# Turning a stage's rows in float32r from a copy made by transfers

## The chip, the cores and the metric

The kernel runs on one core of one Trainium2 chip. Its engines are TensorE (PE, with weight loads shown as PEld), VectorE (DVE), ScalarE (ACT), GpSimd (POOL) and SyncE (SP); each works through its own list of instructions and waits on semaphores. The metric is the device time of one execution in microseconds; lower is better.

## The reference

A model of one sequence of 256 tokens with 1024 features, all float32. Three layers follow each other:

```
h = x
h += attention(rmsnorm(h));           h += relu(rmsnorm(h) @ w1)**2 @ w2      # layer 0: mix0, mlp0
h += rglru_block(rmsnorm(h));         h += relu(rmsnorm(h) @ w1)**2 @ w2      # layer 1: mix1, mlp1
x = rmsnorm(h);  hn = rmsnorm(x)                                              # pre
u = hn @ w_in                                       # 11352 columns: gla, dsa, cross, gates
merged = s_gla*(gla @ w_g) + s_dsa*(dsa @ w_d) + s_mem*(cross(mem) @ w_x)
out = x + rmsnorm(merged @ w_o)
```

What matters here is that the result of each stage has tokens on its rows, and the next product needs it with features on its rows. So between two stages a 256 x 1024 array is turned.

## The kernel before, in words

**Products.** Weights come in tiles of 128 partitions x 2048 float32 (1 MB). `PLAN` is the list of all tiles in the order of their use, `T_OF[name, i]` a tile's place in it. Each tile is cut in two: `hi`, the weights rounded to float32r (ACT, line 852), and `lo = raw - hi` (DVE, line 1379), both by half tiles. The other operand is cut likewise (`xh`, `xl`, side by side in `X2`), and a product is the sum of high x high, low x high and high x low, all in float32r. `raw` has five buffers (`RAW`), `hi` three (`HIS`); `lo` is written over `raw`.

**Loads.** SP issues the load of tile u in plan order, each after the tile five places before is used up (`load`, line 2073 is its `dma_start`). Other transfers of SP stand between two loads at fixed places.

**The order.** PE's instructions are written out by hand. `half(name, i, j, x, b, ks)` makes the 128 output features j of tile i from the blocks `ks` of 8 input feature blocks: a high matmul of 512 columns and a low one of 256 for each. `tokens(name, i, x, banks, ts)` makes tokens x 512 columns from four blocks, three matmuls of 512 columns for each block and each half of the tokens; `rows` is the same for tiles cut by input features. `cols_as_ready` starts a stage: it takes the eight feature blocks in order and waits for each `x_low`. The tiles `mk` and `mv` belong to the product with `mem`, which depends on no stage; they are placed at the stage entries so that PE has work while the stage's input is made.

**Stage entries.** There are five. At mlp0 and mlp1 the rows `h` are turned as soon as DVE has added the stage before (`add_rows`, `h_added`, one increment for 128 tokens x 512 features, order (s 0, c 0), (s 1, c 0), (s 0, c 1), (s 1, c 1)). At mix1 and pre `hn`, the rows times their norm, are turned (`normed`, `hn_made`). At the end `merged` is turned in two halves of the features c. Function `turned` (line 503) waits for the rows, and turns them by 128 x 128 blocks: `PE.transpose` (line 514) with the float32 unit matrix `ident`, four blocks to a bank, two banks to a half c. `turned_x` does both halves. ACT then reads each bank with the norm's gain into `xh` (`x_highs`, line 931), DVE subtracts for `xl` (`x_lows`, line 1415); for `merged` these are `f_highs` (line 1339) and `f_lows` (line 1976). DVE's order at the end is: fl of half 0, `lo` of wf 1, `merged` of half 1 (`to_m`), fl of half 1, then `lo` of wf 2 and wf 3.

Of the kernel before, what the change touches and what calls it, by code (L numbers as in the profile page):

```python
# [8 lines left out]
P = 128  # L9
S = 256  # L10
D = 1024
NC = D // P
F32 = mybir.dt.float32
F32R = mybir.dt.float32r
ALU = mybir.AluOpType
ACT = mybir.ActivationFunctionType
AX = mybir.AxisListType.X

RAW, HIS, BT = 5, 3, 3
# [42 lines left out]
T_OF = {key: t for t, key in enumerate(PLAN)}  # L62
# [28 lines left out]
def build(nc, A, out):  # L91
    ctx = ExitStack()

    def sem(name):
        return ctx.enter_context(nc.semaphore(name))
# [7 lines left out]
    ones_in, vec_in, ident_in, gmask_in, mem_in, h_in = (  # L103
        sem("ones_in"), sem("vec_in"), sem("ident_in"), sem("gmask_in"), sem("mem_in"), sem("h_in"))
# [2 lines left out]
    toep_in, toep2_in, toep_cut = [sem(f"toep_in{i}") for i in range(4)], sem("toep2_in"), sem("toep_cut")  # L107
    first_in, warm_set, kq_scaled, q_scaled, mk_scaled, tok_made = (
        [sem(f"first_in{i}") for i in range(5)], sem("warm_set"), sem("kq_scaled"), sem("q_scaled"), sem("mk_scaled"), sem("tok_made"))
    eps_set, v_step, a_step = sem("eps_set"), sem("v_step"), sem("a_step")  # L110
    x_high, x_low = sem("x_high"), sem("x_low")
    sq_made, sq_added, rstd_made = sem("sq_made"), sem("sq_added"), sem("rstd_made")
# [40 lines left out]
    def slot(name, i, free=(NC, S), dt=F32, off=0):  # L153
        return place(name, o_slot[i] + off, free, dt)

    def small(name, free, dt=F32):
        n = 4
        for f in free:
            n *= f
        return place(name, region((n + 31) // 32 * 32), free, dt)  # L160

    vec = small("vec", [NV])
    ones = small("ones", [P])
    ident = small("ident", [P])
    gmask = small("gmask", [P])
    o_sq = region(4 * 1024)
    o_tmp = region(5 * 1024)
# [77 lines left out]
    gP = slot("gP", 13, [D])  # L245
    fh, fl = slot("fh", 6, dt=F32R), slot("fl", 7, dt=F32R)
    res = slot("res", 9, [2, D])

    bank = [ctx.enter_context(nc.psum_tensor(f"bank{i}", [P, 512], F32)) for i in range(8)]

# [14 lines left out]
    def low_at(name, k_):  # L265
        return NC * SPLITS.index(name) + k_ + 1
# [4 lines left out]
    def pe():  # L271
# [167 lines left out]
            else:  # L439
                used(t, m)  # L440

        def tokens(name, i, x, banks, ts=(0, 1)):
            t = T_OF[name, i]
            c, part = i // 2, i % 2
            wh, wl = hi[t % HIS], lo[t % RAW]
            for s_, k_ in [(s_, k_) for s_ in ts for k_ in range(4)]:
                b = banks[s_]
                if part == 0 and k_ == 0:
                    fill((name, c, s_), b)
                p.wait_ge(lo_cut, cut_at(t, k_ // 2))  # L450
                w, r = slice(k_ * 512, (k_ + 1) * 512), slice(s_ * P, (s_ + 1) * P)
                kk = 4 * part + k_
                m = mm3(bank[b][:, :], x[0][:, kk, r], x[1][:, kk, r], wh[:, w], wl[:, w],
                        part == 0 and k_ == 0, part == 1 and k_ == 3)
                if part and k_ == 3:
                    m.then_inc(filled[b], 1)
            if ts[-1] == 1:
                if part:
                    tile_end[t] = full[name, c, 1]
                else:  # L460
                    used(t, m)
# [41 lines left out]
            PE.matmul(o, V[:, 0, a:b], PT[n % 2][:, 0:256], start=True, stop=False)  # L503
            return PE.matmul(o[:, P:S], V[:, 1, a:b], PT[n % 2][:, 256:384], start=False, stop=True)

        def turned(name, src, c, ready, banks, read):

            p.wait_ge(*ready)
            for m_ in range(2):
                b = banks[m_]  # L510
                done = fill(("turned", name, 2 * c + m_), b, read[m_])
                for e in range(4):
                    j, s_ = 4 * c + 2 * m_ + e // 2, e % 2
                    m = PE.transpose(bank[b][:, e * P:(e + 1) * P], src[:, s_, j * P:(j + 1) * P], ident[:, :])  # L514
                m.then_inc(done, 1)

        def turned_x(name, src, ready, n0):
            for c in range(2):
                turned(name, src, c, (ready, n0 + 2 * c + 2), (2 * c, 2 * c + 1),
                       [(x_low, low_at(name, 4 * c + 1)), (x_low, low_at(name, 4 * c + 3))])  # L520

        X, M = (xh, xl), (mh, ml)

# [68 lines left out]
        def mlp(n, fill_i):  # L592
            p.wait_ge(x_low, low_at("mem", NC - 1))
            half("mk", fill_i, 0, M2, 7)
            turned_x(f"mlp{n}", h, h_added, 8 * n)
            half("mk", fill_i, 1, M2, 6)
            for i in range(17):
                if i == 0:
                    cols_as_ready(f"w1_{n}", 0, X2, (4, 5), f"mlp{n}")
                elif i < 16:  # L600
                    cols_by_part(f"w1_{n}", i, X2, (6, 7) if i == 1 else (4, 5))
                if i > 0:
                    p.wait_ge(z_low, 32 * n + 2 * i)
                    rows(f"w2_{n}", i - 1, 16, zh[(i - 1) % 3], zl[(i - 1) % 3])
# [1 line left out]
        mlp(0, 0)  # L606
        half("mk", 1, 0, M2, 7)
        half("mk", 1, 1, M2, 6)
        half("mk", 2, 0, M2, 4, range(0, 4))
        turned_x("mix1", hn, hn_made, 0)  # L610
        half("mk", 2, 0, M2, 4, range(4, 8))
        half("mk", 2, 1, M2, 5)

        def gates(n):
            p.wait_ge(xc_made, n + 1)
# [19 lines left out]

        tokens("mv", 2, M, (7, 6))
        tokens("mv", 3, M, (7, 6), (0,))
        turned_x("pre", hn, hn_made, 4)
        tokens("mv", 3, M, (7, 6), (1,))

        cols_as_ready("iq", 0, X2, (4, 5), "pre")
        half("misc", 0, 0, X2, 0, last=True)
# [164 lines left out]
        X2_ = (xh2, xl2)  # L807
        for n in range(3):
            tokens("wx", n, X2_, (6, 7) if n < 2 else (4, 5))
        turned("merged", merged, 0, (merged_made, 2), (6, 7), [(f_low, 1), (f_low, 2)])  # L810
        tokens("wx", 3, X2_, (4, 5))

        def last_rows(i):
            p.wait_ge(f_low, i + 1)
            rows("wf", i, 4, fh[:, 2 * i:2 * i + 2, :], fl[:, 2 * i:2 * i + 2, :])

        last_rows(0)
        turned("merged", merged, 1, (merged_made, 4), (4, 5), [(f_low, 3), (f_low, 4)])
        last_rows(1)
        for s_, c in ((0, 0), (0, 1), (1, 0), (1, 1)):  # L820
            r = slice(s_ * P, (s_ + 1) * P)
            for i in (2, 3):
# [9 lines left out]
    def act():  # L832
# [43 lines left out]
        def second(*key, scale=1.0, func=ACT.Copy, **kw):  # L876
            n = len(order)
            order.append(key)
            bt_at[key] = n
            a.wait_ge(*full[key])  # L880
            if n >= BT:
                a.wait_ge(*free[order[n - BT]])
            ACTE.activation(bt[n % BT][:, :], bank_of[key][:, S:2 * S], func, scale=scale, **kw).then_inc(bt_made, 1)  # L883
# [92 lines left out]
        at_tile("wq", 0)  # L976
        for j in range(2):
            second("wq", j, scale=0.125)

        def turned_pair(n):  # L980
            if n >= 2:
# [1083 lines left out]
    def sp():  # L2065
        SP = nc.sync
        s = Side(SP)

        def load(u_):
            name, i = PLAN[u_]  # L2070
            if u_ >= RAW:
                s.wait_ge(*tile_end[u_ - RAW])
            SP.dma_start(raw[u_ % RAW][:, :], A[name][i]).then_inc(raw_in[u_ % RAW], 16)

        SP.dma_start(first[:, :], A["first"][:, 0:3 * S + 16]).then_inc(first_in[0], 16)
        SP.dma_start(second_[:, :], A["second"]).then_inc(first_in[1], 16)
        for k_ in range(3):
            SP.dma_start(front[k_][:, :], A["front"][:, k_, :]).then_inc(first_in[k_ + 2], 16)
        SP.dma_start(hx[:, 4:NC, :], A["xT"]).then_inc(x_in, 16)
        SP.dma_start(vec[:, :], A["vec"]).then_inc(vec_in, 16)  # L2080
        load(2)
        SP.dma_start(ones[:, :], A["ones"]).then_inc(ones_in, 16)
        SP.dma_start(ident[:, :], A["ident"]).then_inc(ident_in, 16)
        SP.dma_start(gmask[:, :], A["gmask"]).then_inc(gmask_in, 16)
        load(3)
        load(4)
        SP.dma_start(mem[:, :, :], A["memT"]).then_inc(mem_in, 16)
        for u_ in range(5, TILES):
            load(u_)
            if 5 <= u_ < 9:  # L2090
                i = u_ - 5
                SP.dma_start(T[:, 4 * i:4 * i + 4, :], A["T"][:, 4 * i:4 * i + 4, :]).then_inc(toep_in[i], 16)
            if u_ == T_OF["wo", 0]:
                SP.dma_start(h[:, :, :], A["x"].rearrange("(s p) d -> p s d", p=P)).then_inc(h_in, 16)
            if u_ == T_OF["w1_0", 8]:
                SP.dma_start(bo[:, :], bass.AP(A["bo"].tensor, 0, [[0, P], [1, D]])).then_inc(bo_in, 16)
            if u_ == T_OF["w1_1", 8]:
                SP.dma_start(gF[:, :], bass.AP(A["gF"].tensor, 0, [[0, P], [1, D]])).then_inc(gf_in, 16)
            if u_ == T_OF["wf", 0]:
                s.wait_ge(ox_gated, 4)  # L2100
                SP.dma_start(gP[:, :], bass.AP(A["gP"].tensor, 0, [[0, P], [1, D]])).then_inc(gp_in, 16)
        for n in range(4):
            s_, r = half_of(n // 2, n % 2)
            s.wait_ge(res_made, n + 1)
            SP.dma_start(out[s_ * P:(s_ + 1) * P, r], res[:, s_, r]).then_inc(out_done, 16)
        s.wait_ge(out_done, 4 * 16)
# [93 lines left out]
```

## Time and profile before

| | |
|---|---|
| three runs | 977.17, 976.54, 976.76 us; median 976.76 |
| profiled execution | 976.28 us, its span 975.0 us |
| mean granted TensorE clock | 0.999 |
| busy | PE 99%, PEld 85%, DVE 70%, ACT 60%, POOL 7% of the span |
| moved | 180.33 MB, 185 GB/s over the span |

The span runs from the first to the last instruction; the profiled execution's time has a little more around it. In a timeline row the instructions of a line that follow each other are put together: the first number is the first one's start, the second reaches from there to the last one's end. A matmul's end is modelled, and matmuls are pipelined: the distance between two starts is what one costs, not its duration.

### The profile page before, as it was taken

What the parts mean: (1) busy time and instruction counts of PE and PEld (TensorE: products, weight loads), DVE (VectorE), ACT (ScalarE), POOL (GpSimd) and SP (SyncE); (2) the same over time, 40 slices, a digit from 0 to 9 for tenths busy, and PEclk for the clock granted to TensorE, in tenths of its full rate; (3) what the DMA queues carried; (4) which work ended last, traced back from release to release, by engine and by line L of the source; (5) the groups of instructions that cost most, each with busy time, mean ns of one, the idle gap of its engine ahead of it and who ended that gap; (6) DMA issues with size and microseconds to landing.
All of it is one profiled execution on the core that took longest, in us unless ns stands there. A gap on an engine that the chain in (4) does not pass through costs nothing.

```text
span 975.0 us, 13399 instructions
## 1 busy us (share of the span) xinstructions
PE 968.3 (99%) x5146; PEld 826.5 (85%) x5146; DVE 680.5 (70%) x1161; ACT 589.0 (60%) x1042; POOL 66.1 (7%) x80
## 2 busy tenths in 40 slices
PE   9999999999999999999999999999999999999997
PEld 6887788888888898888888888888888888988886
DVE  5887776665667789666665688778767554877564
ACT  6777755454456897645454466547876555684443
POOL 1323110000000242000000000000011000000000
PEclk9999999999999999999999999999999999999999
DMA  9753545655455445545555556455553544335551
GB/s 367 301 197 132 181 173 189 222 178 210 173 203 183 148 159 196 182 184 189 222 178 211 173 204 245 171 175 193 194 169 103 195 146 169 133 130 210 175 191 44
DMA packets 27119, 180.33 MB, mean 185 GB/s; under 512 B 2992, under 2 KB 3888, under 8 KB 6320
## 3 DMA queue, kind: packets, MB, share of 16 engines
q1 hardware_dynamic: 26336, 176.98, 50.8%
q0 software_dynamic: 288, 2.10, 0.6%
q8 instruction: 41, 0.67, 0.3%
q10 hardware_dynamic: 432, 0.39, 0.1%
q14 instruction: 22, 0.18, 0.0%
HBM read 178.41 MB, written 1.05 MB: 184 GB/s over the span
## 4 chain that ended last, share of the span: by engine, by line
PE 99%; DMA 1%; DVE 0%; ACT 0%; SPq 0%; issue 0%; DVEq 0%
PE bank L293 16%; PE bank L295 16%; PE bank L294 16%; PE bank L338 14%; PE bank L366 11%; PE bank L346 7%; PE bank L372 6%; PE bank L308 1%; PE bank L498 1%; PE bank L514 1%; PE bank L619 1%; PE bank L548 1%; PE bank L309 1%; PE bank L559 1%; DMA front<-in_front 1%; PE bank L434 0%
## 5 line engine op out<-in xcount | busy, mean ns | idle before, releaser
L1379 DVE TENSOR_TENSOR lo<-raw,hi 128x1024 fp32r<-128x1024 f32 x318 | 376.0, 1230 | 20.1 <-ACT hi L852 19.9
L852 ACT ACTIVATE hi<-raw 128x1024 fp32r<-128x1024 f32 x318 | 320.2, 1050 | 100.1 <-PE bank L295 98.2
L338 PE MATMUL bank<-X,hi 128*128 128x512 f32 x536 | 141.8, 397 | 0.0
L883 ACT ACTIVATE bt<-bank 128x256 f32<-128x256 f32 x135 | 51.2, 382 | 140.6 <-PE bank L372 66.3
L366 PE MATMUL bank<-X,hi 128*128 128x512 f32 x480 | 118.8, 390 | 0.0
L338 PEld LDWEIGHTS bank<-X,hi 128*128 128x128 f32 x536 | 96.7, 189 | 16.9
L366 PEld LDWEIGHTS bank<-X,hi 128*128 128x128 f32 x480 | 90.2, 188 | 17.6
L1393 DVE TENSOR_TENSOR zr<-bank,bt 128x256 f32<-128x256 f32 x64 | 27.2, 424 | 108.4 <-ACT bt L883 108.4
L293 PE MATMUL bank<-hi,zh 128*128 128x512 f32 x256 | 100.0, 390 | 0.0
L295 PE MATMUL bank<-hi,zl 128*128 128x512 f32 x256 | 99.8, 390 | 0.0
L294 PE MATMUL bank<-lo,zh 128*128 128x512 f32 x256 | 99.6, 389 | 0.0
L346 PEld LDWEIGHTS bank<-X,lo 128*128 128x128 f32 x536 | 73.1, 190 | 5.4
L346 PE MATMUL bank<-X,lo 128*128 128x256 f32 x536 | 74.7, 282 | 0.0
L293 PE MATMUL bank<-hi,X 128*128 128x512 f32 (+1 forms) x176 | 67.9, 386 | 0.0
L295 PE MATMUL bank<-hi,X 128*128 128x512 f32 (+1 forms) x176 | 66.9, 380 | 0.0
L294 PE MATMUL bank<-lo,X 128*128 128x512 f32 (+1 forms) x176 | 66.8, 380 | 0.0
L372 PEld LDWEIGHTS bank<-X,lo 128*128 128x128 f32 x480 | 61.5, 191 | 2.3
L372 PE MATMUL bank<-X,lo 128*128 128x256 f32 x480 | 62.3, 283 | 0.0
L295 PEld LDWEIGHTS bank<-hi,zl 128*128 128x128 f32 x256 | 48.1, 188 | 10.4
L294 PEld LDWEIGHTS bank<-lo,zh 128*128 128x128 f32 x256 | 48.1, 188 | 10.2
L293 PEld LDWEIGHTS bank<-hi,zh 128*128 128x128 f32 x256 | 48.2, 188 | 8.9
L1027 ACT ACTIVATE zh<-zf 128x256 fp32r<-128x256 f32 x64 | 26.6, 415 | 21.3 <-DVE zf L1550 21.3
(349 smaller groups left out, 1546.5 us busy)
## 6 DMA issues: line engine op xcount, KB each, us to landing
raw<-in_w SPq DMA_DIRECT2D x64, 1024.0 KB, 4.7
raw<-in_rin SPq DMA_DIRECT2D x8, 1024.0 KB, 4.7
raw<-in_wk SPq DMA_DIRECT2D x4, 1024.0 KB, 10.3
raw<-in_wq SPq DMA_DIRECT2D x4, 1024.0 KB, 8.3
raw<-in_wo SPq DMA_DIRECT2D x4, 1024.0 KB, 4.9
raw<-in_mk SPq DMA_DIRECT2D x4, 1024.0 KB, 4.7
raw<-in_mv SPq DMA_DIRECT2D x4, 1024.0 KB, 4.7
raw<-in_rout SPq DMA_DIRECT2D x4, 1024.0 KB, 4.7
```

The source lines that it names most:

```text
L293: PE.matmul(o, ah, bh, start=start, stop=False)
L294: PE.matmul(o, ah, bl, start=False, stop=False)
L295: return PE.matmul(o, al, bh, start=False, stop=stop)
L338: return PE.matmul(bank[b][:, :], wh[:, c:c + P], x[:, k_, :, :].rearrange("p a b -> p (a b)"), start=k_ == 0, stop=k_ == NC - 1, skip_gro ...
L346: PE.matmul(bank[b][:, 0:S], wl[:, c:c + P], x[:, k_, 0, :], start=False, stop=False, skip_group_check=True)
L366: return PE.matmul(bank[banks[j]][:, :], wh[:, c:c + P], x[:, k_, :, :].rearrange("p a b -> p (a b)"), start=k_ == 0, stop=j == 1 and k_ = ...
L372: return PE.matmul(bank[banks[j]][:, 0:S], wl[:, c:c + P], x[:, k_, 0, :], start=False, stop=j == 0 and k_ == NC - 1, skip_group_check=True)
L852: ACTE.activation(hi[u_ % HIS][:, c], raw[u_ % RAW][:, c], ACT.Copy).then_inc(hi_cut, 1)
L883: ACTE.activation(bt[n % BT][:, :], bank_of[key][:, S:2 * S], func, scale=scale, **kw).then_inc(bt_made, 1)
L1027: ACTE.activation(zh[i % 3][:, j, :], zf[c % 4][:, :], ACT.Copy).then_inc(z_high, 1)
L1379: DVE.tensor_tensor(lo[u_ % RAW][:, c], raw[u_ % RAW][:, c], hi[u_ % HIS][:, c].bitcast(F32), ALU.subtract).then_inc(lo_cut, 1)
L1393: DVE.tensor_tensor(dst, first, rest, ALU.add).then_inc(free[key][0], 1)
```

## The change

A new buffer `moved` (float32r, the size of `h`, in slot 11) takes a copy of the rows at each entry. SP makes it by four transfers of 128 x 512 from SBUF to SBUF, each after its piece of `h`, `hn` or `merged`, with a semaphore for each half c of the features. PE waits for a half's two transfers and turns it with `turner`, a copy of the unit matrix that ACT makes in float32r, into the bank seen as float32r. The two halves of an entry are turned apart, with work of the `mk` or `mv` tile (or `wx`, `wf`) between them, and the turns stand later in PE's order than before: after four blocks of the second half of `mk` at mlp0 and mlp1, after the whole first half of `mk` 2 at mix1, after two blocks more of `mv` 3 at pre, after half of `wx` 3 and half of `wf` 1 for merged.

```diff
+    turner = small("turner", [P], F32R)
+    moved = slot("moved", 11, [2, D], F32R)
...
+        def turned(name, use, c, banks, read):
+            p.wait_ge(rows_moved[c], 32 * use)
             for m_ in range(2):
...
-                    m = PE.transpose(bank[b][:, e * P:(e + 1) * P], src[:, s_, j * P:(j + 1) * P], ident[:, :])
+                    m = PE.transpose(bank[b][:, e * P:(e + 1) * P].bitcast(F32R), moved[:, s_, j * P:(j + 1) * P], turner[:, :])
...
 def mlp(n, fill_i):
             half("mk", fill_i, 0, M2, 7)
-            turned_x(f"mlp{n}", h, h_added, 8 * n)
-            half("mk", fill_i, 1, M2, 6)
+            half("mk", fill_i, 1, M2, 6, range(0, 4))
+            if n == 0:
+                p.wait_ge(turner_made, 1)
+            turned_x(f"mlp{n}", 2 * n + 1, 0)
+            half("mk", fill_i, 1, M2, 6, range(4, 8))
+            turned_x(f"mlp{n}", 2 * n + 1, 1)
...
-        half("mk", 2, 0, M2, 4, range(0, 4))
-        turned_x("mix1", hn, hn_made, 0)
-        half("mk", 2, 0, M2, 4, range(4, 8))
-        half("mk", 2, 1, M2, 5)
+        half("mk", 2, 0, M2, 4)
+        turned_x("mix1", 2, 0)
+        half("mk", 2, 1, M2, 5, range(0, 4))
+        turned_x("mix1", 2, 1)
+        half("mk", 2, 1, M2, 5, range(4, 8))
...
-        turned_x("pre", hn, hn_made, 4)
-        tokens("mv", 3, M, (7, 6), (1,))
+        tokens("mv", 3, M, (7, 6), (1,), range(0, 2))
+        turned_x("pre", 4, 0)
+        tokens("mv", 3, M, (7, 6), (1,), range(2, 4))
+        turned_x("pre", 4, 1)
...
-        turned("merged", merged, 0, (merged_made, 2), (6, 7), [(f_low, 1), (f_low, 2)])
-        tokens("wx", 3, X2_, (4, 5))
+        tokens("wx", 3, X2_, (4, 5), (0,))
+        turned("merged", 5, 0, (6, 7), [(f_low, 1), (f_low, 2)])
+        tokens("wx", 3, X2_, (4, 5), (1,))
...
         last_rows(0)
-        turned("merged", merged, 1, (merged_made, 4), (4, 5), [(f_low, 3), (f_low, 4)])
-        last_rows(1)
+        p.wait_ge(f_low, 2)
+        rows("wf", 1, 4, fh[:, 2:4, :], fl[:, 2:4, :], ks=(0,), last=2)
+        turned("merged", 5, 1, (4, 5), [(f_low, 3), (f_low, 4)])
+        rows("wf", 1, 4, fh[:, 2:4, :], fl[:, 2:4, :], ks=(1,))
...
+        a.wait_ge(ident_in, 16)
+        ACTE.activation(turner[:, :], ident[:, :], ACT.Copy).then_inc(turner_made, 1)
...
+        def move(src, c, ready, n):
+            for s_ in range(2):
+                r = slice(c * 512, (c + 1) * 512)
+                s.wait_ge(ready, n + 2 * c + s_ + 1)
+                SP.dma_start(moved[:, s_, r].bitcast(F32), src[:, s_, r]).then_inc(rows_moved[c], 16)
+
         for u_ in range(5, TILES):
+            for n in range(2):
+                if u_ == T_OF["mk", 3 * n] + RAW:
+                    for c in range(2):
+                        move(h, c, h_added, 8 * n)
+            if u_ == T_OF["mk", 2] + RAW:
+                for c in range(2):
+                    move(hn, c, hn_made, 0)
+            if u_ == T_OF["mv", 3] + RAW:
+                for c in range(2):
+                    move(hn, c, hn_made, 4)
+            if u_ == T_OF["wx", 2] + RAW:
+                move(merged, 0, merged_made, 0)
             load(u_)
...
+        move(merged, 1, merged_made, 0)
```

## Rows read from the trace of the kernel before

**Rows 1.** Page, part 1: busy us, share of the span and instructions of each engine.
```profile
PE 968.3 (99%) x5146; PEld 826.5 (85%) x5146; DVE 680.5 (70%) x1161; ACT 589.0 (60%) x1042; POOL 66.1 (7%) x80
```

**Rows 2.** Page, part 4: chain that ended last, shares of the span by engine.
```profile
PE 99%; DMA 1%; DVE 0%; ACT 0%; SPq 0%; issue 0%; DVEq 0%
```

**Rows 3.** Waits of PE: who it waited for, total us, times, longest us.
```profile
PE bank L526 <- POOL warm L2025: 1.3, 1, 1.3
PE bank L408 <- ACT hi L950: 0.3, 1, 0.3
```

**Rows 4.** Groups by form: shape, count | busy us, mean ns of one | idle before.
```profile
L338 PE MATMUL bank<-X,hi 128*128 128x512 f32 x536 | 141.8, 397 | 0.0
...
L346 PE MATMUL bank<-X,lo 128*128 128x256 f32 x536 | 74.7, 282 | 0.0
...
L491 PE MATMUL bank<-dk,dq 128*128 128x128 f32 x16 | 3.1, 274 | 0.0
...
L338 PEld LDWEIGHTS bank<-X,hi 128*128 128x128 f32 x536 | 96.7, 189 | 16.9
```

**Rows 5.** Line 514, the turns: duration ns min/median/max, first and last start.
```profile
L514 PEld LDWEIGHTS bank<-ident,h x32: 139/140/142, 118.9 to 402.1; 128*128 128x128 f32 x32
L514 PE MATMUL bank<-ident,h x32: 272/273/273, 119.1 to 402.2; 128*128 128x128 f32 x32
```

**Rows 6.** Timeline of PE, entry mlp0: start us, us from first start to last end.
```profile
119.09 1.91 PE L514 MATMUL bank<-ident,h 128*128 128x128 f32 x16
120.76 1.85 PE L338 MATMUL bank<-M,hi 128*128 128x512 f32 x7
122.44 1.12 PE L346 MATMUL bank<-M,lo 128*128 128x256 f32 x8
...
123.63 0.40 PE L308 MATMUL bank<-X,hi 128*128 128x512 f32 x1
```

**Rows 7.** Timeline of PE, entries mix1 and pre.
```profile
305.19 1.09 PE L338 MATMUL bank<-M,hi 128*128 128x512 f32 x4
...
589.51 1.91 PE L514 MATMUL bank<-ident,hn 128*128 128x128 f32 x16
```

**Rows 8.** Timeline of SP's queue: the loads just before four entries.
```profile
116.52 0.33 SPq L2073 DMA_DIRECT2D raw<-in_w  x1
...
305.62 0.33 SPq L2073 DMA_DIRECT2D raw<-in_rin  x1
...
398.01 0.33 SPq L2073 DMA_DIRECT2D raw<-in_w  x1
...
586.99 0.33 SPq L2073 DMA_DIRECT2D raw<-in_dk  x1
```

**Rows 9.** DMA issues: count, KB each, median us from issue to landing.
```profile
raw<-in_w SPq DMA_DIRECT2D x64, 1024.0 KB, 4.7
...
h<-in_x SPq DMA_DIRECT2D x1, 1024.0 KB, 6.9
...
out<-res SPq DMA_DIRECT2D x4, 256.0 KB, 2.0
...
gP<-in_gP SPq DMA_DIRECT2D x1, 512.0 KB, 5.9
```

**Rows 10.** Timeline of DVE: what the turns of mlp0, mix1 and pre read.
```profile
116.25 2.48 DVE L1425 TENSOR_TENSOR h<-bank,h 128x512 f32<-128x512 f32 x4
...
304.96 1.67 DVE L1444 TENSOR_SCALAR hn<-h,nst 128x512 f32<-128x512 f32 x4
...
588.48 1.68 DVE L1444 TENSOR_SCALAR hn<-u,nst 128x512 f32<-128x512 f32 x4
```

**Rows 11.** Timeline of DVE and PE, the last turn.
```profile
949.01 0.69 DVE L1869 TENSOR_TENSOR merged<-merged,PT 128x512 f32<-128x512 f32 x1
...
955.01 4.62 DVE L1379 TENSOR_TENSOR lo<-raw,hi 128x1024 fp32r<-128x1024 f32 x4
...
952.54 1.03 PE L514 MATMUL bank<-ident,merged 128*128 128x128 f32 x8
```

More of the change, by code:

```diff
@@ L109, in build @@
         [sem(f"first_in{i}") for i in range(5)], sem("warm_set"), sem("kq_scaled"), sem("q_scaled"), sem("mk_scaled"), sem("tok_made"))
+    turner_made, rows_moved = sem("turner_made"), [sem(f"rows_moved{c}") for c in range(2)]
     eps_set, v_step, a_step = sem("eps_set"), sem("v_step"), sem("a_step")
@@ L440, in value_rows, with tokens @@
                 used(t, m)
-        def tokens(name, i, x, banks, ts=(0, 1)):
+        def tokens(name, i, x, banks, ts=(0, 1), ks=range(4)):
             t = T_OF[name, i]
@@ L445, in tokens @@
             wh, wl = hi[t % HIS], lo[t % RAW]
-            for s_, k_ in [(s_, k_) for s_ in ts for k_ in range(4)]:
+            for s_, k_ in [(s_, k_) for s_ in ts for k_ in ks]:
                 b = banks[s_]
@@ L456, in tokens @@
                     m.then_inc(filled[b], 1)
-            if ts[-1] == 1:
+            if ts[-1] == 1 and ks[-1] == 3:
                 if part:
@@ L504, in weigh @@
             return PE.matmul(o[:, P:S], V[:, 1, a:b], PT[n % 2][:, 256:384], start=False, stop=True)
-        def turned(name, src, c, ready, banks, read):
-            p.wait_ge(*ready)
+        def turned(name, use, c, banks, read):
+            p.wait_ge(rows_moved[c], 32 * use)
             for m_ in range(2):
@@ L513, in turned, with turned_x @@
                     j, s_ = 4 * c + 2 * m_ + e // 2, e % 2
-                    m = PE.transpose(bank[b][:, e * P:(e + 1) * P], src[:, s_, j * P:(j + 1) * P], ident[:, :])
+                    m = PE.transpose(bank[b][:, e * P:(e + 1) * P].bitcast(F32R), moved[:, s_, j * P:(j + 1) * P], turner[:, :])
                 m.then_inc(done, 1)
[L517 to L520, printed above, removed]
+        def turned_x(name, use, c):
+            turned(name, use, c, (2 * c, 2 * c + 1), [(x_low, low_at(name, 4 * c + 1)), (x_low, low_at(name, 4 * c + 3))])
         X, M = (xh, xl), (mh, ml)
```

## The prediction

> **What bounds the kernel now.** I read the busy shares first, then the chain of waits, then PE's own waits, and last the timelines around the six places where rows are turned. PE works 968.3 of 975.0 us [rows 1], the chain that ended last is PE for 99% of the span [rows 2], and PE waits for another engine only twice, for 1.6 us, both in the first 10 us [rows 3]. So the kernel is one unbroken stream of PE instructions: each nanosecond taken out of the stream is won, each stall put into it is paid in full, and all that the other engines do counts only where it comes too late for PE. In these rows the reader is to see that no stage has slack on PE, and so what matters of a new wait is the work that PE has ahead of it.
>
> **The turns themselves.** 80 transposes are changed (16 in each of mlp0, mix1, mlp1, pre and merged). Sixteen start at 119.09 and the next matmul at 120.76: 104 ns each [rows 6]. The half after them takes 2.87 us against 2.80 of its parts (8 matmuls of 512 columns at 0.23, which is (1.09-0.39)/3, and 8 of 256 at 0.12, from the 1.12 that 8 of them last: (1.12-0.28)/7) [rows 6, 7], so some 0.08 us is lost at each of the 6 places where transposes give way to float32r matmuls; I count 0.5 us that may go. No row shows a float32r instruction of 128 columns. Floor: float32r instructions of 512 and 256 columns differ by 115 ns, so 128 columns stream in 58 ns, where plain float32 ones need 104 (that form lasts 274, the transpose 273) [rows 4, 5]. Ceiling: nothing in float32r follows its predecessor faster than the 0.12 us of the 256 column matmuls, and their weight loads last 189 ns where the transposes' last 140 [rows 4, 5]; if the load decides, a transpose takes 0.12. An ordinary float32 matmul of 128 columns is two instructions (L491 has 16 for its 8 calls [rows 4]), 0.21 us: the end of what is thinkable, 8.5 us more. Neither near row decides between 58 and 104-120, so I take 82 ns: 80 x 0.022 + 0.5 = 2.3 us won. Bounds: 4.2 won, 1.3 lost (the 8.5 as a rare case).
>
> The Trainium skill ("TensorE: Matmul & The Clock Gate", section "LDWEIGHTS (loading the stationary operand)") speaks against the gain: loading weights takes columns over 1.2 GHz, whatever the rows, an estimate of 107 ns for the 128 columns here. The trace's transposes follow each other at 104 ns, so today's rows agree with it as they do with streaming. By that rule nothing of the 1.8 us would be won.
>
> **The copies.** PE's turn used to wait for h or hn itself; now it waits for two transfers of 256 KB for each half of the features (four for a whole entry), issued by SP. What decides is what stands ahead of them in SP's queue. The loop issues the transfers of mlp0 before the load of tile mk+5, so right behind the load of tile mk+4, a full megabyte which goes out when the last tile of the stage before has ended: at 116.52, 305.62, 398.01 and 586.99 [rows 8]. Such a load lands 4.7 us after its issue. gP (512 KB, issued just behind a load) lands 5.9 us after its own issue and h<-x (1 MB, likewise) 6.9; a lone 256 KB store lands in 2.0 [rows 9]. If the queue shared its rate between the two, gP would be in at about 4.7; it isn't, so a transfer runs after the one ahead. From h: 6.9 + 0.4 (its later issue) - 4.7 = 2.6 us for a megabyte, 0.65 for 256 KB. So the first half of the features (two transfers) is there 4.7 + 1.3 = 6.0 us after the load's issue, the second 7.3 us after. Their data are ready earlier: the fourth h ends at 118.73, the fourth hn of mix1 at 306.63 [rows 10].
>
> - mlp0: ready at 116.52 + 6.0 = 122.5. PE has, after the half that ended at 119.09, only four of eight k of the next half: 1.4 us, to 120.5. Stall 2.0. The second copy (123.8) is covered: 0.7 of turning and 1.4 of the other four k lead to 124.6.
> - mlp1 repeats it: 398.01 + 6.0 = 404.0. Its last transpose starts at 402.2 [rows 5], its first so at 400.6, and 400.6 + 1.4 = 402.0. Stall 2.0.
> - mix1: the turn now stands after the whole first half of mk 2, which starts at 305.19 + 0.23 and takes 2.8: 308.2 [rows 7]. The load is issued at 305.62, the copies are in at 311.6. Stall 3.4.
> - pre: 6 matmuls of 0.23 after 589.51 [rows 7]: 590.9; the copies are in at 593.0. Stall 2.1 (hn is complete at 590.2 [rows 10], so the load ahead is what is late, not the norm).
>
> Sum 9.5, and at each of the four PE starts anew: 0.2 us (the lead of a weight load over its matmul, the 189 ns of [rows 4]), +0.8. What is late next behind these stalls is nothing: ACT's eight scaled copies and DVE's eight subtractions follow the turns by some 3 us as before, and the k order of the next tile needs the fifth feature block 2.8 us after its start. The closest is mix1, where DVE still has half a tile of rin to cut behind them; 0.9 us is left by my count.
>
> SP's own queue: while it waits for h or hn nothing is behind it but the load of tile mk+5, which waits for the end of mk anyhow, so no load starts later for the wait. 20 more issues of 0.33 us lie where SP idles. In ACT's queue one 128x128 copy at the wq stage, some 0.25 us, hidden as PE waits for ACT nowhere there.
>
> **merged.** The first copy goes behind a wf load that was issued when wx 1 ended, 5.5 us before wx 2 ends, and PE now has half of wx 3 (2.8 us) more ahead of the turn: covered by over 1 us. The second has no load before it for 10 us. Its data, complete at 949.7 today [rows 11], come 1.3 later because DVE's fl for the first half does (turn 2.8 later, but DVE was behind by 1.5); 951.0 and 2.0 to 2.6 us make 953.0 to 953.6, and PE comes to it only after half of wf 1, at 952.54 + 2.8 - 0.3 = 955.0: covered. But the moved turn makes DVE late. It subtracts for fl (two instructions) and only then cuts the last four half tiles of wf, 4.62 us from 955.01, 2.47 after the turn began [rows 11]. Before, there was all of wf 1 (24 matmuls, 5.5 us) to cover this. After, PE turns at 955.0 and has half of it (12 matmuls, 2.8 us) from 955.7, so to 958.5. DVE begins on them at 957.3 (955.0 + 2.47, less 0.2 of turning), they are ready at 958.5, 959.6, 960.8 and 961.9; PE wants one each 0.7 us: 958.5, 959.2, 959.9, 960.6. The last comes 1.3 us late, with 0.2 to start anew: +1.5.
>
> Against the profiled execution's own 976.28 us (span 975.0): +9.5 +0.8 +1.5 -2.3 = +9.5, 985.8. The three runs' median is 0.5 above the profiled one; I forecast 986.2.
>
> **Bounds of the copies.** No row shows a transfer from SBUF to SBUF. Below: if they come behind the load for nothing (0 instead of 1.3), the four stalls are 4.3 in place of 9.5 (5.2 less). Above: at half the load's rate the first copies come 1.3 later and the second too are late by some 0.4 at each entry: 6.8 more.
>
> **The rivals.**
> - *Weights decide* (the page's rule as a mechanism of this kernel): a turn is 0.104 to 0.12 as before, so of the gain 0.5 is left or 1.3 is lost: 988.0 to 989.8. For it: 189 against 140 ns of load. Against: today's transposes load in 140, a form that float32r ones may keep. Chance 0.13. The skill's page above gives 107 ns for it.
> - *Slow copies*: half rate, 992.7. For it: both ends are in SBUF and rows are 2 KB where the loads' are 8 KB. Chance 0.10.
> - *Not slower, the other side*: the transfers don't run behind the load but beside it, at 2.0 to 2.6 us after the data. Then mlp0, mlp1 and mix1 are covered (data of the first half at 117.5 + 2.6 = 120.1 against 120.5), pre pays 1.0 and merged 1.5. With turns at 82 ns that is +0.2, no change, 976.8; with turns at the 58 ns floor -1.7, 975.0. It decides from a queue delay below 1.5 us. For it: 16 engines that could take small packets between large ones. Against: gP's 5.9. Chance of the first 0.05, of the second 0.10, and 0.03 more that merged's stall isn't there either, 973.5.
> - *The gate*: the granted clock is full in the profile before (0.999), where PE never stood; a stand of 3.6 us at mix1 could let it fall from 2.4 to 1.2 GHz, and then matmuls are spaced twice 0.23 for a few us: 2 to 4 more, 989. Chance 0.05.
> - *Four passes*: float32r of 128 columns at the price of the ordinary float32 matmul, 994.5. Chance 0.03.
>
> **Numbers.** The forecast has the remaining 0.51, and by itself 982 to 989.5. Its spread is the turns' price (-1.9, +1.8) and the copies' (-3 to +2). What a measurement of this kernel can tell from no change is 0.2%, 2.0 us. Faster 0.08 (half of the floor case, which lies near the bound, and the 0.03), same 0.10 (its other half and the 0.05), slower 0.82. The range for 8 in 10: 979.5 to 993; it leaves the other side out, and the four-pass case.
>
> **What would show it.** In the profile after: PE waits for the transfers into moved four times, longest at mix1 (3.4), 2.0 to 2.1 at the others, and once for DVE's lo near 960; landing times of the moved transfers of 3 to 6 us at four entries, but 2 to 2.6 in the last one; transposes 60 to 100 ns apart; PE busy below 968. The prediction is wrong if PE shows no waits for the transfers, if they land within 3 us behind a load, or if the turn's spacing is over 0.12.

## The result

The kernel after takes 999.36 us, median of 5 runs (998.34 to 999.89), against 976.76 us before (5 runs, 976.36 to 977.17): a ratio of 1.0231, 95% interval 1.0220 to 1.0243, slower by 22.6 us. The forecast was 986.2 us, range 979.5 to 993: the sign was right, the size less than half. The profiled execution took 998.36 us (span 996.9), 22.1 more than the one before (976.28, span 975.0); the ledger below is made between these two.

The page of the kernel after: parts 1, 2 and 4, to be set against [rows 1, 2] (in part 2 the clock stood at 9 in all 40 slices before).

```profile
PE 974.4 (98%) x5146; PEld 829.0 (83%) x5146; DVE 680.6 (68%) x1161; ACT 589.8 (59%) x1043; POOL 65.0 (7%) x80
...
PEclk9999999999998999999999999999999999999999
...
PE 92%; DVE 3%; DMA 2%; ACT 1%; issue 1%; SPq 0%; DVEq 0%; ACTq 0%
```

PE has the same 5146 instructions, of which 80 should be shorter, and yet is busy 6 us longer: the first sign that something beside waiting went wrong. The chain leaves PE for 8% of the span where it was 1%. PE's waits after (against [rows 3]); line 517 is the turn:

```profile
PE bank L517 <- DMA moved<-hn: 7.5, 2, 5.1
PE bank L517 <- issue: 3.6, 1, 3.6
PE bank L517 <- DMA moved<-h: 3.5, 1, 3.5
...
PE bank L296 <- DVE lo L1393: 0.3, 1, 0.3
```

Four waits for the copies, as forecast; the one put down to "issue" is mlp0's, and ends when its copies land. Next PE's timeline at the entries mlp0, mix1, mlp1 and pre (against [rows 6, 7]):

```profile
120.47 0.40 PE L341 MATMUL bank<-M,hi 128*128 128x512 f32 x1
124.51 0.93 PE L517 MATMUL bank<-turner,moved 128*128 128x128 f32 x8 [3.64 <-issue]
125.23 1.61 PE L341 MATMUL bank<-M,hi 128*128 128x512 f32 x3
...
127.92 1.00 PE L517 MATMUL bank<-turner,moved 128*128 128x128 f32 x8
...
313.16 0.39 PE L341 MATMUL bank<-M,hi 128*128 128x512 f32 x1
318.60 1.25 PE L517 MATMUL bank<-turner,moved 128*128 128x128 f32 x8 [5.05 <-DMA moved<-hn]
...
322.34 1.04 PE L517 MATMUL bank<-turner,moved 128*128 128x128 f32 x8
...
413.67 0.40 PE L341 MATMUL bank<-M,hi 128*128 128x512 f32 x1
417.59 0.89 PE L517 MATMUL bank<-turner,moved 128*128 128x128 f32 x8 [3.52 <-DMA moved<-h]
...
420.75 1.17 PE L517 MATMUL bank<-turner,moved 128*128 128x128 f32 x8
...
607.35 0.39 PE L298 MATMUL bank<-hi,M 128*128 128x512 f32 x1
610.18 1.26 PE L517 MATMUL bank<-turner,moved 128*128 128x128 f32 x8 [2.44 <-DMA moved<-hn]
...
613.59 0.80 PE L517 MATMUL bank<-turner,moved 128*128 128x128 f32 x8
```

A matmul of 512 columns costs 0.23, so PE stands 3.8, 5.2, 3.7 and 2.6 us: 15.3 in all, where the forecast had 10.3 (9.5 and 0.8 to start anew). And behind the stall of mlp0 the half of a half, 1.40 us of work, takes from 125.23 to 127.92, 2.69 us. The windows say why (columns: stretch, length, busy time and instructions of PE, PEld, DVE, ACT, POOL, then the granted clock, DMA share and GB/s):

```profile
120.50:124.50 4.00, 0.37 (x3) 0.07 (x2) 0.42 (x1) 1.40 (x3) 0.71 (x1) 1.00 0.92 317
...
125.00:128.50 3.50, 3.50 (x18) 3.03 (x17) 1.66 (x4) 1.57 (x4) 0.00 (x0) 0.51 0.02 6
...
609.50:610.00 0.50, 0.00 (x0) 0.00 (x0) 0.00 (x0) 0.00 (x0) 0.00 (x0) 0.76 1.08 414
```

The granted clock falls from full to 0.5 (2.4 to 1.2 GHz) at each of the four entries. At mlp0 and mlp1 it falls 0.6 and 1.0 us after PE has begun again, and stays low for 3.4 us. At mix1 and pre it falls while PE still stands (the last row is pre's, where PE begins at 610.18): at mix1 for 6.8 us, of which 2.4 lie in the stall, at pre for 3.4, of which 0.4. Next, SP's queue at mlp0, and what was landed there, with the time from issue to landing; the last two rows are the same view of the entry mix1 (against [rows 8, 9]):

```profile
116.73 0.33 SPq L2087 DMA_DIRECT2D raw<-in_w  x1
117.17 2.77 SPq L2107 DMA_DIRECT2D moved<-h  x4
```

```profile
raw<-in_w SPq DMA_DIRECT2D x1, 1024.0 KB, 6.4
moved<-h SPq DMA_DIRECT2D x4, 256.0 KB, 6.4
...
raw<-in_rin SPq DMA_DIRECT2D x1, 1024.0 KB, 6.5
moved<-hn SPq DMA_DIRECT2D x4, 256.0 KB, 6.6
```

The load in front of the copies, 4.7 us in [rows 9], takes 6.4 and 6.5 here, 6.3 at mlp1 and 5.1 at pre: the copies not only wait for it, they make it longer.

**Ledger of the span (us).** Stalls 15.3; slow clock 6.4 (the matmuls between the two turns of an entry 4.6, the turns 1.8); the end 1.6; turns at full clock -1.9; start 0.2. Sum 21.6 of 21.9. The 4.6 is what the matmuls between two turns take beyond their 1.40 us (1.36 at pre): 1.29, 1.29, 1.03 and 0.99. The 1.8 is what the eight groups of turns there take beyond the 0.64 us of one at the full clock.

### The profile page after: what moved, and what is told of

Read it like the earlier page. It is cut to its first block, busy times and chain, and to the rows that moved or that the text cites. A ratio compares the mean times of both kernels' runs of the same rounds, so it can differ in the third digit from the quotient of the medians.

```text
span 996.9 us, 13424 instructions
## 1 busy us (share of the span) xinstructions
PE 974.4 (98%) x5146; PEld 829.0 (83%) x5146; DVE 680.6 (68%) x1161; ACT 589.8 (59%) x1043; POOL 65.0 (7%) x80
## 3 DMA queue, kind: packets, MB, share of 16 engines
HBM read 178.41 MB, written 1.05 MB: 180 GB/s over the span
## 4 chain that ended last, share of the span: by engine, by line
PE 92%; DVE 3%; DMA 2%; ACT 1%; issue 1%; SPq 0%; DVEq 0%; ACTq 0%
PE bank L296 15%; PE bank L298 14%; PE bank L297 14%; PE bank L341 13%; PE bank L369 11%; PE bank L349 7%; PE bank L375 6%; DVE lo L1393 2%; PE bank L311 1%; PE bank L501 1%; DMA moved<-hn 1%; PE bank L517 1%; PE bank L625 1%; PE bank L549 1%; DMA moved<-h 1%
```

## The experiments

Each ran beside the kernel before on its chip, whose median was 976.47 (e1 to e4), 976.90 (e5 to e8) and 976.72 (e9 to e12); the ratio has its 95% interval behind it. Twelve runs, ten kernels.

**e1, the turns alone.** `hR`, `hnR` and `mergedR` are the same bytes as the rows, seen as float32r. The order is that of before, nothing is copied.

```diff
-                    m = PE.transpose(bank[b][:, e * P:(e + 1) * P], src[:, s_, j * P:(j + 1) * P], ident[:, :])
+                    m = PE.transpose(bank[b][:, e * P:(e + 1) * P].bitcast(F32R), src[:, s_, j * P:(j + 1) * P], turner[:, :])
...
-        turned_x("mix1", hn, hn_made, 0)
+        turned_x("mix1", hnR, hn_made, 0)
```

> The kernel before, its order and its waits, with the 80 turns in float32r straight from h, hn and merged (each seen a second time as float32r at the same address); no copies. If the turn itself got cheaper in the changed kernel (80 ns apart at the full clock in its last entry against 104), this run wins 80 x 0.024 + up to 0.5 of the hand-over: 974.4 us, 2.3 below the kernel before. Rival: the 80 ns come from the copy or the place and the weights decide; then it is the kernel before, 976.8.

Measured 974.69 us, 0.9981 [0.9973, 0.9990]; again as e11 below. PE at mlp0:

```profile
119.48 1.48 PE L517 MATMUL bank<-turner,hR 128*128 128x128 f32 x16
120.79 0.93 PE L341 MATMUL bank<-M,hi 128*128 128x512 f32 x3
```

Sixteen turns in 1.31 us, 82 ns each, against 104 [rows 6]. The price of a turn was right, and the copy is not needed for it.

**e2, the order alone.** The kernel after with its places in PE's order, but turned in float32 from the rows themselves, with no copies.

```diff
-            p.wait_ge(rows_moved[c], 32 * use)
+            src, ready, n0 = SRC[name]
+            p.wait_ge(ready, n0 + 2 * c + 2)
```

> The changed kernel's order of PE with float32 turns straight from the rows: no copies, PE waits for h, hn or merged themselves. My theory says the new places cost only the end, where DVE cuts the last tiles of wf too late (1.7 us in the changed kernel, 1.9 here as the turns are longer): 978.6. Rival: the new places by themselves carry a good part of the 22.6 us; then over 981, with waits of PE at the entries.

Measured 977.92, 1.0017 [1.0008, 1.0026], 0.7 below what I expected. PE waits at no entry. What is left stands at the end (DVE, then PE on wf 1 and wf 2):

```profile
956.90 4.62 DVE L1396 TENSOR_TENSOR lo<-raw,hi 128x1024 fp32r<-128x1024 f32 x4
```

```profile
958.26 0.47 PE L296 MATMUL bank<-hi,fh 128*128 128x512 f32 x1
...
959.31 0.50 PE L296 MATMUL bank<-hi,fh 128*128 128x512 f32 x1
...
960.53 0.47 PE L296 MATMUL bank<-hi,fh 128*128 128x512 f32 x1 [0.26 <-DVE lo L1396]
...
961.57 0.50 PE L296 MATMUL bank<-hi,fh 128*128 128x512 f32 x1
```

A group of three matmuls is 0.68 us, and here their starts are 1.05, 1.22 and 1.04 apart: PE keeps DVE's pace of 1.16 us for a half tile. The view of waits names only 0.3 us of this, since most of the loss hides in short gaps; the distance of starts is the row to read.

**e3, PE kept at work.** The kernel after with spare matmuls of 512 columns in front of the wait, 14, 20, 14 and 9 at the four entries, which do nothing for the result.

```diff
+                if m_ == 0 and not c and name in SPARE:
+                    for _ in range(SPARE[name]):
+                        PE.matmul(bank[b][:, :], M2[:, 0, 0, 0:P], M2[:, 0, :, :].rearrange("p a b -> p (a b)"), start=True, stop=True, skip_group_check=True)
+                    p.wait_ge(rows_moved[c], 32 * use)
```

> The changed kernel with 14, 20, 14 and 9 spare matmuls of 512 columns into the free bank just before PE's wait for the first half of a copy at mlp0, mix1, mlp1 and pre (their results are overwritten by the turn). The copies come as late as before. If the lower clock after the four waits is a cost of its own, it goes: 4.6 us of the matmuls behind and 1.8 of the turns, to 993.0, with a granted clock of 1.00 in all four places. If it is only a sign of the waits: 999.4.

Measured 992.64, 1.0171 [1.0157, 1.0185]: some 6 us below the kernel after (spans 990.8 and 996.9), with the same transfers behind the same load.

```profile
119.44 3.37 PE L520 MATMUL bank<-M 128*128 128x512 f32 x14
123.26 0.88 PE L524 MATMUL bank<-turner,moved 128*128 128x128 f32 x8 [0.45 <-DMA moved<-h]
123.97 0.93 PE L341 MATMUL bank<-M,hi 128*128 128x512 f32 x3
...
125.45 0.80 PE L524 MATMUL bank<-turner,moved 128*128 128x128 f32 x8
```

The half of a half now takes 1.48 (123.97 to 125.45) in place of 2.69, and the granted clock is 1.00 throughout. So the 6.4 us of the ledger are the clock's, shown by taking it away; the 6.1 between the spans is if anything low, since at mlp1 a copy landed later and PE turned 9.0 us after the load's issue in place of 7.7. The Trainium skill ("TensorE: Matmul & The Clock Gate", section "HAM oscillation — how this bites in real kernels") tells of a kernel in which PE starts each step at the slow clock after waiting for a transfer. The trace of after agrees at mix1 and pre, where PE began again at 0.50; at mlp0 and mlp1 it began at 1.00, and the clock fell only behind that.

**e4, the copies ahead of the load.** One tile earlier in SP's loop, so that they are issued before the 1 MB load in place of behind it.

```diff
-                if u_ == T_OF["mk", 3 * n] + RAW:
+                if u_ == T_OF["mk", 3 * n] + RAW - 1:
...
-            if u_ == T_OF["mk", 2] + RAW:
+            if u_ == T_OF["mk", 2] + RAW - 1:
...
-            if u_ == T_OF["mv", 3] + RAW:
+            if u_ == T_OF["mv", 3] + RAW - 1:
```

> The changed kernel with each entry's four copies issued before the 1 MB load that stood ahead of them (for merged before wf 2). Theory: they were late because they ran behind that load; alone they land 2.2 to 2.6 us after their data. Then mlp0 and mlp1 have no wait, mix1 0.4, pre 1.2, the clock stays, the end keeps its 1.7: 978.5. Rival (copies from SBUF to SBUF are slow in themselves): waits of 2 us and more stay at all four entries and the time stays above 990.

Measured 978.68, 1.0026 [1.0016, 1.0035]: some 20 of the 22.6 us are gone. Waits for the copies:

```profile
PE bank L517 <- DMA moved<-hn: 1.5, 2, 1.0
```

The clock stays at 1.00. So both large terms, stalls and clock, hang on one thing: the load of 1 MB in front. That the load itself goes out 2.8 us later (119.57 in place of 116.73) shows no cost in any row.

**e5, a queue of their own.** The 16 copies of the four entries issued by ACT.

```diff
+        def move(src, n, ready, n0):
+            s_, r = half_of(n % 2, n // 2)
+            a.wait_ge(ready, n0 + n + 1)
+            ACTE.dma_start(moved[:, s_, r].bitcast(F32), src[:, s_, r]).then_inc(rows_moved[n // 2], 16)
```

> The kernel after with the 16 copies of mlp0, mix1, mlp1 and pre issued by ACT on its own DMA queue, each as soon as its piece of h or hn is made; merged's copies stay on SP. In the kernel after they stand on SP's queue behind a 1 MB load issued a moment earlier and land 7.6 to 7.8 us after that load's issue at mlp0. If the place in SP's queue is what makes them late, a queue of their own lets them share the 16 DMA engines with the load: they should land 3 to 5 us after their issue, stalls at the four entries fall from 15.3 us to about 3, and the time to 980 to 984 us (with a new cost: ACT spends about half a microsecond on each issue, in front of its squares). If the engines' total rate sets it instead, whichever the queue, the landings stay at 6 to 7 us after the issue and the time at 995 to 999 us.

Measured 994.26, 1.0178 [1.0164, 1.0192]. At mlp0, issue to landing:

```profile
raw<-in_w SPq DMA_DIRECT2D x1, 1024.0 KB, 6.5
moved<-h ACTq DMA_DIRECT2D x4, 256.0 KB, 6.4
```

Theory missed, rival right at three entries: a queue of their own changes neither number. Only at mlp1 did they come earlier: there ACT issued the first two copies before the load (409.04 and 409.91 against 410.28), and PE stood 1.2 us, for the second half alone, at a clock that held. This makes most of the 5 us by which the kernel is below after, and puts the time just below the rival's range. The Trainium skill ("DMA: Bandwidth & Descriptors", section "Issuing engines are not separate DMA queues") says that a second issuing engine saves only the time of issuing; the trace agrees, 6.4 us either way.

**e6, from DRAM.** Copies of the same shape, order and waits, but read from the input x, so that the kernel leaves the copying of the rows out; moved and turned in float32.

```diff
-                SP.dma_start(moved[:, s_, r].bitcast(F32), src[:, s_, r]).then_inc(rows_moved[c], 16)
+                rows_ = src[:, s_, r] if ready is merged_made else A["x"][s_ * P:(s_ + 1) * P, r]
+                SP.dma_start(moved[:, s_, r], rows_).then_inc(rows_moved[c], 16)
```

> The kernel after with the 16 copies of the four entries reading a piece of the input x of the same shape from DRAM instead of h or hn from SBUF (the turned data are wrong there: this kernel leaves the copying of the rows out), moved and turned in float32. Order, waits, sizes and packets' length stay. It tells whether SBUF as the source is what stretches the load in front of the copies. Theory A (reading SBUF costs nothing of its own; two transfers that share an engine's queue slow each other): landings at mlp0 again 7.3 to 8 us after the load's issue, the load's packets again near 0.50 us, total 999 to 1002 us (float32 turns add some 1.5). Theory B (SBUF source is slower): landings near 6.0, load's packets near 0.37, stalls 5 us shorter in all, 993 to 996 us.

Measured 993.30, 1.0168 [1.0154, 1.0182]: just inside theory B's range, but not by its sum alone. The stalls are 12.1 us in all, 3.3 shorter and not 5, and the clock fell at two entries (mlp0, mix1) in place of four. At mlp0 and, below, at mix1:

```profile
raw<-in_w SPq DMA_DIRECT2D x1, 1024.0 KB, 4.8
moved<-in_x SPq DMA_DIRECT2D x4, 256.0 KB, 5.4
...
raw<-in_rin SPq DMA_DIRECT2D x1, 1024.0 KB, 4.8
moved<-in_x SPq DMA_DIRECT2D x4, 256.0 KB, 5.7
```

The load is back at its 4.8 us (4.7 to 4.9 at all four entries), and PE turns 6.5 us after the load's issue (116.39, 122.89) in place of 7.8. So it is the source in SBUF, not a transfer behind it as such, that stretches the load. A second thing shows: PE stood 3.1 us at pre (603.63 + 0.23 to 606.92) with the clock at 1.00 behind it, while the kernel of e5 stood 2.3 there (603.90 + 0.23 to 606.47) and the clock fell:

```profile
606.90:609.90 3.00, 2.98 (x21) 2.68 (x22) 1.41 (x4) 1.59 (x5) 0.00 (x0) 1.00 0.14 52
```

```profile
606.40:609.40 3.00, 2.93 (x13) 2.55 (x14) 1.48 (x4) 1.57 (x4) 0.00 (x0) 0.59 0.21 79
```

Within e6 itself the clock fell behind the stall of 2.5 us at mlp0 and not behind the 2.4 at mlp1 or the 3.1 at pre. Between stalls of such lengths the length alone doesn't tell whether the clock falls.

**e7 and e9, fewer and longer packets.** One transfer of 1 MB with 8 KB rows (e7), or two of 512 KB with 4 KB rows (e9), in place of four with 2 KB rows; PE waits for all of it before the first turn.

```diff
+                s.wait_ge(ready, n + 4)
+                SP.dma_start(moved[:, :, :].rearrange("p a b -> p (a b)").bitcast(F32), src[:, :, :].rearrange("p a b -> p (a b)")).then_inc(rows_moved[1], 16)
```

```diff
+                s.wait_ge(ready, n + 3 + c)
+                SP.dma_start(moved[:, c, :].bitcast(F32), src[:, c, :]).then_inc(rows_moved[c], 16)
```

> The kernel after with one transfer of 1 MB (packets of 8 KB, 128 of them, like a load's) in place of the four of 256 KB (512 packets of 2 KB) at each of the four entries; PE waits for it before either half. If it is the many small packets and their four issues that stretch the load ahead, then the load keeps its 0.37 us a packet, and the copy lands about 2.6 us after the load, at 7.5 us after its issue: the first half no later than in the kernel after, stalls 14 to 16 us in all, and the time 997 to 1000 us with the load unstretched. If any transfer queued behind the load stretches it, load and copy end together at 8.5 to 9 us after the issue: the first stall of each entry is 1 to 1.5 us longer and the time 1001 to 1005 us.

> The kernel after with two transfers of 512 KB (256 packets of 4 KB, one for each half of the tokens) in place of the four of 256 KB (2 KB packets) at each of the four entries; PE waits for both before either half. In the kernel after, the 8 KB packets of the load ahead took 0.51 us each at mlp0; with one copy in 8 KB packets they took 0.31 us as in the kernel before, and with four copies in 2 KB packets out of DRAM also 0.31 to 0.34. Theory: what stretches the load is short packets read from SBUF, and it scales with their number: with 4 KB packets the load's take about 0.38 to 0.42 us, the copies land 8 to 8.5 us after the load's issue, time 1000 to 1002 us. Rival: it is the number of issues in front of the load's end, not the packets' length: two issues late in the load leave its packets at 0.31 us, landing at 7.6, time 999 to 1000 us.

Measured 1001.72 (1.0254 [1.0240, 1.0268]) and 1004.08 (1.0280 [1.0266, 1.0295]). Landings at mlp0, e7 and then e9, and below them e7 at mlp1:

```profile
raw<-in_w SPq DMA_DIRECT2D x1, 1024.0 KB, 4.9
moved<-h SPq DMA_DIRECT2D x1, 1024.0 KB, 5.1
```

```profile
raw<-in_w SPq DMA_DIRECT2D x1, 1024.0 KB, 5.2
moved<-h SPq DMA_DIRECT2D x2, 512.0 KB, 5.1
```

```profile
raw<-in_w SPq DMA_DIRECT2D x1, 1024.0 KB, 6.3
moved<-h SPq DMA_DIRECT2D x1, 1024.0 KB, 8.1
```

At mlp0 the load is nearly unhurt, 4.9 and 5.2, and PE turned 7.4 us after its issue in e7 (7.5 expected) and 7.9 in e9 (8 to 8.5, rival 7.6). Taken alone, this speaks for the theory that short packets or many issues stretch the load. But both times are above their theory's (e7's lies in its rival's range), and mlp1 speaks against it: there e7's one copy with 8 KB rows was issued 0.7 us behind the load (410.65 against 409.93), and the load took 6.3 us, as it did with four copies in after.

What goes with the stretch at every entry of after, e7 and e9 is how soon behind the load the first copy out of SBUF is issued:

| first copy issued behind the load, us | the load from issue to landing, us |
|---|---|
| 0.4 (after at mlp0, mix1, mlp1; e9 at mlp1) | 6.4, 6.5, 6.3; 6.3 |
| 0.6 (e9 at mix1), 0.7 (e7 at mlp1) | 6.2, 6.3 |
| 1.0 (e7 at mix1) | 5.6 |
| 1.6 (e9 at mlp0) | 5.2 |
| 2.0 (after at pre), 2.2 (e7 at mlp0) | 5.1, 4.9 |
| 2.8 (e9 at pre), 3.2 (e7 at pre) | 4.6, 4.7 |

In these rows the number and the length of the packets show no effect of their own. No run changed the delay alone, so it is read from twelve entries and not shown by an experiment. (Where e9's expectation sets 0.51 us a packet against 0.31, it sets a mean beside a median: the means are 0.51 in after and 0.37 in before, the medians 0.42 and 0.31.)

As for the times, I had left out that these transfers can be issued only when the last piece of the rows is there, or the third in e9 (119.63 in e7, where the first of four went out at 117.17 in after), and that both turns of an entry now wait for all: PE stands 17.6 us in e7 and 18.5 in e9, and the slow clock lasts 6.8 us at mlp1 and pre, where it lasted 3.4 in after.

**e10, DVE's order at the end.** The kernel of e4, with the low part of wf 2 made before fl of half 1.

```diff
         to_m("wx", 1)
+        lo_to(2 * TILES - 2)
         f_lows(1)
         lo_to(2 * TILES)
```

> The kernel of e4 (kernel after with the copies of the four entries issued ahead of the 1 MB load; 978.68 us, 1.0026 of before) with one more change: DVE makes the low part of wf 2 before the low parts of merged's second half, instead of after. It tests the last term of the forecast, DVE's lateness at the end. Theory: the 1.5 to 1.7 us that PE waits there for the low parts goes, 977.1 us, ratio about 1.001. Rival: then PE waits as long for fl of half 1, which is late in its place: 978.7.

Measured 977.38, 1.0008 [0.9999, 1.0017], 1.3 us below e4, or 1.5 when each is set against its own kernel before, and PE's wait for `lo` is out of its list. The forecast's last term is shown: it was DVE's order, and free to mend. Turns from a copy then cost nothing that can be told from no change, and win nothing either.

**e8, e11 and e12, all turns in float32r.** The kernel of e1, and with it the 88 turns of the softmax rows and 16 of the gated output.

```diff
-                m = PE.transpose(bank[b][:, dst:dst + P], L[n % 2][:, src:src + P], ident[:, :])
+                m = PE.transpose(bank[b][:, dst:dst + P].bitcast(F32R), LR[n % 2][:, src:src + P], turner[:, :])
...
-                    m = PE.transpose(bank[b][:, m_ * 256 + j * P:m_ * 256 + j * P + P], og[:, j, c:c + P], ident[:, :])
+                    m = PE.transpose(bank[b][:, m_ * 256 + j * P:m_ * 256 + j * P + P].bitcast(F32R), ogR[:, j, c:c + P], turner[:, :])
```

> The kernel of e1 (kernel before, turns in float32r straight from h, hn and merged, no copies; 974.69 us, 0.9981 of before) and the 88 turns of the attention's softmax rows and 16 of the gated output og in float32r too. Theory: every turn is set by the matmul's own passes, so each goes from about 104 ns to about 80: 104 x 0.024 = 2.5 us further, 972.2 us, ratio about 0.9955. Rival: these turns stand in groups of two to four between matmuls, where the engine waits for something else, so they win nothing: 974.7, ratio 0.998.

> The kernel of e1 again (kernel before, the 80 turns of the entries in float32r straight from the rows, no copies), beside the kernel with all turns in float32r on one chip: ratio 0.998 to before, about 974.7.

> The kernel of e8 again (also the 104 turns of the attention in float32r), beside the one with only the entries' turns in float32r, on one chip: if the short groups win as the long ones do, it is 1.0 to 2.0 us below that kernel; if its margin in e8 came from the chip, the two are equal within 0.5 us.

Measured: e8 973.69, 0.9969 [0.9957, 0.9981]; on one chip e11 975.06, 0.9982 [0.9974, 0.9991], and e12 973.63, 0.9969 [0.9958, 0.9980]. The short groups win too, 1.4 us for 104 turns, somewhat over half of what 24 ns each would give. The groups of the softmax turns, before and in e12 (busy us, mean ns of one):

```profile
L498 PE MATMUL bank<-ident,L 128*128 128x128 f32 x88 | 14.5, 278 | 0.0
```

```profile
L505 PE MATMUL bank<-turner,LR 128*128 128x128 f32 x88 | 12.1, 250 | 0.0
```

That is less than the 2.5 expected in e8. This kernel beats both: it is 3.1 us below the one before on its chip, and some 26 below the one after.

## Why the prediction was wrong

**The copies' landing: the step that failed.** It said that the first half is there "4.7 + 1.3 = 6.0 us after the load's issue". PE turned 7.8, 7.8, 7.7 and 6.5 us after it. The 1.3 for two copies behind the load held (7.8 less the load's 6.4 is 1.4); the 4.7 did not, since copies out of SBUF issued 0.4 us behind a load stretch it to 6.3 to 6.5, and the same copies out of DRAM do not (after, e6). At pre the copies are issued 2.0 us behind the load (605.69 to 603.68), which then lands in 5.1, and the term is 0.5 off. Over four entries the stalls are 5.0 us more than the 10.3 forecast: 5.8 for the late landings, and 0.8 less because the 0.2 us to start anew at each entry isn't there (PE turned 0.1 us or less after the landing). I had gP and h<-x to go by, both read from DRAM; I read from them that a transfer waits for the one ahead, and took for granted that it leaves that one as it was. For these two it does: in the trace of before the loads ahead of them landed in 5.0 and 4.8 us. No row of before had a transfer out of SBUF behind a load. Of the bounds, the upper one (half rate, 6.8 us more) came close to these 5.0 for a reason that didn't hold.

**The clock: a rival priced too low.** It was given 0.05, for mix1 alone, at 2 to 4 us. It fell at all four entries, also at the 2.6 us of pre, and cost 6.4 us (e3: some 6). It is also why the sign "PE busy below 968" failed (974.4). The trace of before had no stall of PE to read it from, but the forecast itself put four of 2.0 to 3.4 us into a stream that had never stood, and counted the fall for one of them. Each stall was taken as its own length.

**The order of landing.** That copies wait for the load ahead was right: e4 removes some 20 us by this alone. The other side ("beside it, at 2.0 to 2.6 us") is refuted, even on another queue (e5).

**The turns.** 82 ns forecast; 82 at mlp0 in e1, and 80 at the last in after, where eight take from 975.70 to 976.34. That the middle between floor and ceiling was met is luck: the forecast chose it because no row decided. 2.3 us forecast, 1.9 in the ledger, 1.8 and 1.7 in the medians of e1 and e11. The weights' rule, 107 ns, and its rival are refuted: the load instructions of the new turns last as long as those of [rows 5], 137 ns at least and 144 in the middle, and yet follow each other at 80. The short loss where turns give way to matmuls stayed, which is the 0.4 too much. In the same view as [rows 5]:

```profile
L517 PEld LDWEIGHTS bank<-turner,moved x80: 137/144/223, 124.5 to 976.2; 128*128 128x128 f32 x80
L517 PE MATMUL bank<-turner,moved x80: 222/255/369, 124.5 to 976.3; 128*128 128x128 f32 x80
```

**merged.** No stall for the copies, right; the last two landed 2.2 us after their issue, where no load was ahead of them. DVE late by 1.5 forecast, 1.6 measured: in after five groups of wf, from 978.48 to 983.50, take 5.02 us for 3.4 of work. Right in size, cause and place (e2, e10), and DVE's row answers [rows 11]:

```profile
978.03 4.62 DVE L1393 TENSOR_TENSOR lo<-raw,hi 128x1024 fp32r<-128x1024 f32 x4
```

**The sum.** Forecast +9.5; measured +22.1 in the profiled executions. The difference of 12.6 is 5.0 of stalls, 6.4 of clock, 0.4 of turns, 0.1 of the end, 0.2 of the start, and 0.5 not placed. The range took its upper end from slow copies alone. With the 6.4 measured for the clock added, the centre would have been 992.6 and the case of slow copies 999.4. Two rivals' sums are off by the prediction's own terms: slow copies give 986.2 + 6.8 = 993.0, not 992.7, and four passes 986.2 + 1.8 + 8.5 = 996.5, not 994.5. Neither bears on the outcome.

## What to carry to other kernels

Before a copy is added so that an operand has another type, see whether the same bytes can be read under that type: here that was the whole gain (974.7, and 973.6 with all turns), and the copy, behind a load, the loss. Where a transfer must be waited for, put it in front of large loads in the order of issue, not behind them, whichever queue it is on; some 20 us hung on that. And price a stall put into a PE that never stood as its length plus the slow clock behind it: here 15.3 us of stalls brought 6.4 more, though with stalls of 12.1 us the clock fell at only two entries of four (e6).

## What was not expected of the hardware

- A 1 MB load from DRAM that takes 4.8 us takes 6.4 when four 256 KB copies out of SBUF with 2 KB rows are issued 0.4 us behind it, 6.5 when they are on another queue, and 4.8 when the same copies read DRAM. One copy of 1 MB with 8 KB rows stretches it as much when it is issued 0.7 us behind (6.3, e7 at mlp1), and hardly when it is issued 2.2 us behind (4.9, e7 at mlp0). Why reading SBUF does this stays open.
- In after the granted clock was 0.5 for 3.4 us at three of the stalls and for 6.8 at mix1, and the fall came 2.4 and 0.4 us before PE began again (mix1, pre) or 0.6 and 1.0 us after (mlp0, mlp1). Behind a stall of 3.1 us it did not fall (e6), and behind one of 2.3 it did (e5).
- A float32r turn of 128 columns follows the one before at 80 to 82 ns, although its weight load lasts some 140.
